# Splitting the projection work between attention steps into parts of two matmuls, and moving what follows VectorE some steps later

## What is computed

```python
proj = h @ w_in[layer]                       # q | k | v | u | gates
# branch A: 8 heads of 64, blocks of 256 keys, top 3 past blocks per query
gate = einsum('bhqd,bhnd->bhqn', qc, k_mean)
gate = where(arange(nb) < own, gate, NEG_INF)
_, sel = lax.top_k(gate, k_sel)
p = softmax(concat([s_sel, s_own])).astype(v.dtype)
y_a = (p_sel @ v_g + p_own @ v_own) @ w_branch_a
# branch B: trailing means of 2, 4, 8, 16 tokens, minus the token
mixed = window_sum / count - u
y_b = (einsum('bsgc,gcd->bsgd', mixed, w_pool) * pool_scale) @ w_branch_b
x = x + (sigmoid(g0) * y_a + sigmoid(g1) * y_b) @ w_out
```

## Time and profile before

| | |
|---|---|
| median of 3 runs | 2349.37 us (2342.2 to 2542.82) |
| profiled execution, device time | 2344.48 us |
| its span (first to last instruction, slowest core) | 2343.4 us |
| spans of the eight cores | 2335.9 to 2343.4 us |
| mean granted TensorE clock, core 1 | 0.934 |
| busy: TensorE, VectorE, ScalarE | 2000.3, 1254.0, 833.8 us |
| first attention stage (layer 1) | 83.9 to 457 us |
| second attention stage (layer 2) | 1211 to 1592 us |

### The profile page before, as it was taken

How to read it: one execution, slowest core, us unless ns; L and a number is a source line. 1 busy time by engine, 2 the same in 40 slices (tenths; PEclk the granted TensorE clock), 3 DMA queues, 4 the chain that set the end, 5 groups by cost and what they waited for, 6 DMA issues and landing times.

```text
span 2343.4 us, 32398 instructions; the slowest of 8 cores (2335.9 to 2343.4 us)
## 1 busy us (share of the span) xinstructions
PE 2000.3 (85%) x12288; PEld 978.8 (42%) x12288; DVE 1254.0 (54%) x1700; ACT 833.8 (36%) x1015; POOL 124.9 (5%) x240
## 2 busy tenths in 40 slices
PE   1867766899999899899996777779999899999987
PEld 1534433444444344344463434334445444444434
DVE  3534333243468748758773324333336785685776
ACT  3344444522234304224434443443223441340443
POOL 1000000000000000000010000000000000000000
PEclk9988887899999999999998878769999999999999
DMA  8101010022132222222130010102222322223213
GB/s 203 19 5 19 1 19 10 5 41 41 28 42 36 32 37 34 35 40 31 15 58 5 1 19 1 18 10 32 37 33 32 45 33 36 36 28 45 33 18 144
DMA packets 38663, 79.60 MB, mean 34 GB/s; under 512 B 4320, under 2 KB 8544, under 8 KB 38496
## 3 DMA queue, kind: packets, MB, share of 16 engines
q0 software_dynamic: 33760, 60.39, 18.2%
q1 hardware_dynamic: 4752, 17.15, 2.2%
HBM read 129.51 MB, written 8.39 MB: 59 GB/s over the span
## 4 chain that ended last, share of the span: by engine, by line
PE 71%; DVE 13%; ACT 7%; issue 6%; DMA 2%; SPq 0%; DVEq 0%; ACTq 0%
PE ps L467 38%; PE ps L912 12%; DVE tv L894 4%; PE ps L858 4%; PE ps L703 4%; ACT Pt L721 4%; PE ps L738 3%; PE ps L808 2%; PE ps L805 2%; PE ps L501 2%; ACT tv L890 2%; DMA xs<-xt 2%; DVE hs L462 1%; DVE tA L576 1%; DVE kz L488 1%
## 5 line engine op out<-in xcount | busy, mean ns | idle before, releaser
L467 PE MATMUL ps<-hs,ring 128*128 128x512 bf16 x4608 | 1097.0, 397 | 59.3 <-DVE tv L894 46.3
L467 PEld LDWEIGHTS ps<-hs,ring 128*128 128x128 bf16 x4608 | 462.8, 102 | 653.5 <-issue 170.8
L912 PE MATMUL ps<-hid,ring 128*128 128x512 bf16 x1408 | 311.9, 383 | 16.5 <-DVE hid L903 15.1
L721 ACT ACTIVATE Pt<-ps 128x1024 bf16<-128x1024 f32 x320 | 271.8, 894 | 90.4 <-PE ps L703 33.3
L894 DVE SCALAR_TENSOR_TENSOR tv<-ps,pv,tv 128x1024 f32<-128x1024 f32 (+2 forms) x176 | 225.8, 1283 | 118.9 <-ACT tv L890 109.4
L738 PE MATMUL ps<-Vt,Pt 128*128 128x65 bf16 x2176 | 132.2, 205 | 152.7 <-ACT Pt L721 146.1
L894 DVE SCALAR_TENSOR_TENSOR tg<-ps,pv,tg 128x1024 f32<-128x1024 f32 (+2 forms) x176 | 225.0, 1279 | 32.5 <-ACT tg L890 22.9
L912 PEld LDWEIGHTS ps<-hid,ring 128*128 128x128 bf16 x1408 | 138.0, 99 | 185.3 <-issue 26.6
L703 PE MATMUL ps<-qz,kz 72*128 72x512 bf16 (+3 forms) x640 | 206.2, 397 | 10.5 <-DVE qz L657 10.5
L738 PEld LDWEIGHTS ps<-Vt,Pt 128*128 128x128 bf16 x2176 | 110.6, 106 | 241.3 <-issue 224.2
L900 ACT ACTIVATE tg<-tg 128x1024 f32<-128x1024 f32 x88 | 93.1, 1058 | 317.7 <-DVE tg L894 317.6
(11 more groups left out here) (78 smaller groups left out, 1299.4 us busy)
## 6 DMA issues: line engine op xcount, KB each, us to landing
ring<-w_up POOLq DMA_DIRECT2D x88, 256.0 KB, 3.8
ring<-w_in POOLq DMA_DIRECT2D x64, 256.0 KB, 4.5
xs<-xt SPq DMA_DIRECT2D x16, 512.0 KB, 27.0
yt<-yst SPq DMA_DIRECT2D x16, 512.0 KB, 2.6
ring<-w_down POOLq DMA_DIRECT2D x32, 224.0 KB, 3.6
ring<-w_ab POOLq DMA_DIRECT2D x16, 256.0 KB, 4.6
ring<-w_out POOLq DMA_DIRECT2D x16, 256.0 KB, 4.7
ring<-w_down POOLq DMA_DIRECT2D x16, 256.0 KB, 3.8
```

The costliest lines, as they stand in the source:

```text
L467: S.op("pe", lambda e: [e.matmul(bank(b), w[:, kc, :], hs[:, c, kc, :], start=(kc == 0), stop=(kc == 7)) for kc in range(8)][-1], reads=[r ...
L721: S.op("act", lambda e: e.activation(Pt[:, pi, 0:n], ps[:, sl * 1024:sl * 1024 + n], AF.Exp, scale=0.125), reads=[PB[2 * sl], PB[2 * sl + ...
L912: S.op("pe", lambda e: [e.matmul(bank(b), w[:, kc, :], hid[:, kc, c * 512:(c + 1) * 512], start=(kc == 0), stop=(kc == nk - 1)) for kc in ...
```

## The change

Each `q`, `k`, `v` and `u` unit is now four parts (`pieces`, `mm8_part`, `proj_v_part`): two matmuls of 512 columns each, or eight of 128 for `v`. The parts of a unit fill one bank over some steps; only behind the last part do the copies out of the bank follow, on the same engines as before. A part counts 0.45 and a `gA` 0.4, and a window's parts are spread by the scores of each step (0.5 plus scores/1024), so a small step gets half as much as a full one. The windows are also filled differently: 6 `u` units now stand in the pairs 0 to 2 and 10 in pair 3, where they were 9 and 7; in pair 3 VectorE copies `u` out of the bank instead of ScalarE.

What depends on VectorE goes on a list (`later`) and is issued by `run_due` some steps on, just before `values(s)`: the sums of `u`, two instructions a step; the ranking in three groups on the three steps after `gA`; `um` two steps after `mx`, `gB` two steps after the ranking, `tr` three steps (not two) after the head's end. One entry of the list with TensorE work is issued in a step. These short tasks use the bank that the latest unit doesn't (`short_bank`).

```diff
 def m1_plan():
-    cnt = [(0, 1, 2), (0, 1, 2), (0, 1, 2), (2, 2, 3)]
+    cnt = [(0, 0, 2), (0, 0, 2), (0, 0, 2), (3, 3, 4)]
...
-COST = {"gA": 0.8, "gB": 0.3, "q": 1.73, "k": 1.73, "v": 1.8, "u": 1.95}
...
+        def mm8_part(b, w, rw, c, lo, hi):
+            S.op("pe", lambda e: [e.matmul(bank(b), w[:, kc, :], hs[:, c, kc, :],
+                                           start=(kc == 0), stop=(kc == 7)) for kc in range(lo, hi)][-1],
+                 reads=[rw] + R_h[c][lo:hi], writes=[PB[b]])
...
+            def run_due(tag=None, all_=False, pe_too=True):
+
+                used = False
+                for it in list(todo):
+                    if tag is not None:
+                        ok = it[1] == tag
+                    else:
+                        ok = all_ or (it[0] <= now[0] and not (it[2] and (used or not pe_too)))
+                    if ok:
+                        todo.remove(it)
+                        used = used or it[2]
+                        it[3]()
...
+                ops.append(mixin)
+                for k, f in enumerate(ops):
+                    later(1 + k // 2, "ud", False, f)
...
+                    later(2, "gB%d" % c, True, lambda: gate_b(m, c))
+                for k, f in enumerate((compare, ties, choose)):
+                    later(1 + k, "gd", False, f)
...
+                    mm8_part(b, w, rw, c, 2 * k, 2 * k + 2)
+                    if k < 3:
+                        return
+                    if kind == "u":
+                        u_done(m, c, b, now[0] >= 120)
+                        return
...
+                return [(0.45, lambda k=k: part(k)) for k in range(4)]
...
-                        trq.append([s + 2, tr])
+                        later(3, "tr", True, tr)
...
-                    q = list(plan[m][w])
-                    tot = sum(COST[t[0]] for t in q)
+                    q = [p for t in plan[m][w] for p in pieces(t)]
+                    room = [0.5 + sum(x[2] for x in steps[40 * m + s][5]) / 1024.0 for s in range(a, z)]
+                    tot = sum(p[0] for p in q)
                     for s in range(a, z):
-                        starts[40 * m + s] = (q, tot * (z - 1 - s) / (z - a))
+                        when[40 * m + s] = (q, tot * sum(room[s - a + 1:]) / sum(room))
```

More of the change, by code:

```diff
@@ L185, in m1_plan @@
     ut = [(g, c) for g in (3, 2, 1, 0) for c in range(NCH)]
-    cnt = [(0, 1, 2), (0, 1, 2), (0, 1, 2), (2, 2, 3)]
+    cnt = [(0, 0, 2), (0, 0, 2), (0, 0, 2), (3, 3, 4)]
     for m in range(4):
-        def us(n):
-            return [("u",) + ut.pop(0) for _ in range(n)]
+        us = [[("u",) + ut.pop(0) for _ in range(n)] for n in cnt[m]]
+        nxt = m + 1 if m < 3 else None
         w0 = [("gA", m, 2)]
@@ L192, in m1_plan @@
             w0.append(("q", m, 3))
[L193 to L206, removed]
+        if nxt:
+            w0 += [("v", nxt, 0), ("v", nxt, 1)]
+        w0 += us[0][:1] + [("gA", m, 3)] + us[0][1:]
+        if nxt:
+            w0.append(("v", nxt, 2))
+        w1 = []
+        if nxt:
+            w1 += [("v", nxt, 3)] + [("k", nxt, c) for c in range(NCH)]
+        w1 += us[1]
+        w2 = [("q", nxt, c) for c in range(3)] if nxt else []
+        w2 += us[2]
         segs.append((w0, w1, w2))
     return segs
-COST = {"gA": 0.8, "gB": 0.3, "q": 1.73, "k": 1.73, "v": 1.8, "u": 1.95}
 def load_order():
@@ L498, in fn @@
                 ins = None
-                for t4 in range(4):
+                for t4 in range(lo, hi):
                     for kc in range(8):
@@ L521, in mixer, with long_bank, short_bank, later @@
             fctr = [0]
-            def fb():
+            now = [0]
+            todo = []
+            def long_bank():
                 fctr[0] += 1
                 return 6 + fctr[0] % 2
+            def short_bank():
+                return 6 + (fctr[0] + 1) % 2
+            def later(n, tag, pe, fn):
+                todo.append((now[0] + n, tag, pe, fn))
+            def run_due(tag=None, all_=False, pe_too=True):
[9 more added lines that the diff above has]
+                        it[3]()
             for st in range(2):
@@ L659, in gate_b, with pieces, part @@
                          reads=[PB[b]], writes=[R_q[c]])
[L661 removed]
+            def pieces(t):
                 kind = t[0]
[L663 to L675 removed]
+                if kind == "gA":
+                    return [(0.4, lambda: gate_a(t[1], t[2]))]
+                m, c = t[1], t[2]
+                box = []
+                def part(k):
+                    if k == 0:
+                        box.append(long_bank())
+                    b = box[0]
+                    if kind == "v":
+                        proj_v_part(l, m, c, b, k, k + 1)
+                        return
+                    w, rw = W(l, kind, m)
+                    mm8_part(b, w, rw, c, 2 * k, 2 * k + 2)
+                    if k < 3:
+                        return
+                    if kind == "u":
+                        u_done(m, c, b, now[0] >= 120)
+                        return
                     if c == 3:
@@ L753, in tr @@
                         def tr():
[L754 removed]
+                            b = short_bank()
                             trb = bank(b).bitcast(BF16)
@@ L779, in mixer @@
                 attend(s)
-                while trq and trq[0][0] <= s:
-                    trq.pop(0)[1]()
-                if s in starts:
-                    q, left = starts[s]
-                    while q and sum(COST[t[0]] for t in q) > left + 1e-6:
-                        task(q.pop(0))
+                if s in when:
+                    q, left = when[s]
+                    while q and sum(p[0] for p in q) > left + 0.2:
+                        q.pop(0)[1]()
+                run_due()
                 values(s)
-            while pend_um:
-                pend_um.pop(0)()
-            while trq:
-                trq.pop(0)[1]()
+            while todo:
+                run_due(all_=True)
             heir("mg", ["kqv"])
```

130 lines of the change are left out of this document (65 added, 65 removed).

## The result

The changed kernel takes **2149.26 us** (median of 4 runs, 2148.25 to 2149.9). Against the kernel before on the same chip the ratio is **0.9162** (95% interval 0.9137 to 0.9186): 8.4% faster. The profiled execution took 2149.47 us, 195 us less than the one before.

A forecast was written before the change was run, and what follows sets the result against it. Attention stages were taken as bound by TensorE's waits and lower clock, no engine being full. Work 405.6 + waits 126 + clock 29 = 561 us for 754, so 2344.5 - 194 = 2150 us; range 2100 to 2240.

The forecast's parts named there:

- run-out: A TensorE matmul before a wait shows its full run-out: 0.15 us for each of some 165 waits before, 25 us.
- work at full clock: TensorE's work in both attention stages, start to start at full clock: 405.6 us, the same matmuls after the change.
- values waiting for Exp: TensorE's values waiting in the attention stages: 66 us behind `q` and `k` units, 10 behind `u`, 31 behind `um`.
- all other waits: TensorE's remaining waits in both stages: `gA` 8 x 1.0, `gB` and scores behind it 6 x 1.0, stages' ends 5: 19 us.
- lower clock: Time both stages lose to TensorE's reduced clock: 118 us before; most should go, a quarter, 29 us, is kept.
- rival B: Waits only move: ScalarE's order is the true bound and short tasks wait for banks; 2336 us, chance 0.07.
- The copies of `u` moved to VectorE: 20 of 32 `u` copies go to VectorE, adding 14 us of work there; costed at 0, as VectorE is busy 36%.
- The `q` and `k` holes: Behind each of 48 units the 2.84 us copy-and-Exp chain stays, more matmuls cover it: mean wait 1.37, 66 us for 103.
- the term of 31 us: Values behind `um`: a chain of 2.33 us against 1.34 of cover, 0.99 us for each of 32.
- 312 signals: Units issued in four operations signal 312 times more: taken as 0; by the Trainium skill 8 us higher.
- Rival A: The clock doesn't come back: waits fall as forecast but the 118 us of lower clock stay; 2240 us, chance 0.14.
- C: Slower, as the lower clock becomes lasting: the stages run at 0.50 and take 831 us; 2421 us, chance 0.05.

The follow-up runs named there:

- ScalarE first: Changed kernel, but ScalarE copies the first head of each `q` or `k` unit and VectorE the second: 2122.52 us, ratio 0.9048.

## What the prediction had right, and the step that failed

The forecast was 2150 us and 194 us of gain; measured were 2149.3 and, in the profiled executions, 195. The mechanism is shown: the chain behind a unit stays, the parts cover it, and the clock follows. That the total came out to 1 us is luck, for the waits were mis-sized both ways, by some 40 us, and cancel. By the prediction's own reckoning, with 0.15 us of run-out for each of the 133 waits:

| term, both stages | before | predicted | measured |
|---|---|---|---|
| work at full clock | 405.6 | 405.6 | 405.6 (the same instructions) |
| values waiting for Exp | | 107 | 56.7 + 10 = 67 |
| all other waits | | 19 | 52.0 + 10 = 62 |
| waits together | 231 | 126 | 129 |
| lower clock | 118 | 29 | 20 (what is left) |
| stages | 754 | 561 | 555 |

**The step that failed** is the term of 19 us for all other waits: they took 52.0 us idle and some 62 with run-out. The 68 waits behind it, in idle us of both stages, against what the prediction had for them:

| wait of TensorE | predicted | measured |
|---|---|---|
| `gA` for the casts of the key sums, 8 | 8 | 10.0 |
| `gB` for the bank of a `v` unit, 8; scores behind a `gB`, none | 6 | 4.1 |
| at the stages' ends, 4 | 5 | 3.4 |
| `tr` for the bank of a `q` unit that ScalarE still copies, 6 | 0 | 7.1 |
| `um` and parts behind VectorE's queue in pair 3, 8 | 0 | 10.2 |
| a part or a short task whose bank the last short task's reader still holds, 34 | 0 | 16.4 |

What the prediction priced came out near its price. It put at nothing that parts and short tasks share banks 6 and 7, so that each waits until the one before it in its bank is read. It argued that few short tasks stand in the step in which a unit ended, and priced such waits in rival B alone; the trace has 40 of them (the fourth and the last line), of 0.2 to 1.7 us. And it took VectorE as covered because it is busy 36% on the mean. That is the mean of a stage: at the start of pair 3, where ranking, sums, copies and divisions meet, VectorE was the bound. Most of the 40 are not of this kind: in some 18 of their 23.5 us the reading engine had been idle and began at once, and TensorE waited for as long as the reading lasts. The copies of `u` moved to VectorE were costed at 0, with a gain of some 16 us on ScalarE's side, and gave nothing, since on ScalarE they leave no wait for an Exp either.

**The `q` and `k` holes**: the chain stays, its cover grows. Right, shown from both sides: without the parts the waits for Exp are back at 62 us a stage, and with ScalarE first the wait shrinks by 0.9 us, the VectorE copy of 0.68 and its hand-over. The size was too large: 66 us predicted for 48 holes; 36 of the units have a wait of values behind them, 41.7 us idle and 47 with run-out. They run from 0.69 to 1.76 us, against 0.88 to 1.74 predicted, so one hole was sized well and their number wasn't: behind six more units it is the `tr` above that waits.

**`um`**: the term of 31 us was too large. Values wait behind 17 of the 32, 0.3 to 1.0 us each, 9.6 us in all:

```profile
329.13 0.38 PE L627 MATMUL ps<-mx,wpl 128*128 128x512 bf16 x1
329.61 0.69 ACT L629 ACTIVATE pooledT<-ps,pv 128x512 bf16<-128x512 f32 x1 [0.55 <-PE ps L627]
330.19 1.93 ACT L774 ACTIVATE Pt<-ps 128x1024 bf16<-128x1024 f32 x2
330.44 0.59 PE L468 MATMUL ps<-hs,ring 128*128 128x512 bf16 x2 [0.25 <-ACT pooledT L629]
331.35 0.41 PE L791 MATMUL ps<-Vt,Pt 128*128 128x65 bf16 x8 [0.32 <-ACT Pt L774]
```

The chain is 2.22 us as priced (2.33), but here the wait is 0.57 in two places. Behind the others no value waits for its Exp.

**The work** and the signals: taken as 0, and right. The 8 us that the prediction held against the split for 312 signals are not there, by the unit of 1.73 us with four signals above.

**The clock**: most of the 118 us came back, as predicted; a quarter was kept for what turned out to be a sixth. The 20 us are what is left of the sum, and the granted clock agrees: at 0.95 and 0.96 some 50 us of the stages run at the lower level, where the same work takes twice the time, so by estimate up to 25 us. Where the clock is still lost TensorE had mostly waited for VectorE just before. At the start of pair 1:

```profile
148.94 0.34 PE L650 MATMUL ps<-ksb,qz 72*128 72x8 bf16 x8 [1.39 <-DVE ksb L642]
149.75 0.59 PE L468 MATMUL ps<-hs,ring 128*128 128x512 bf16 x2 [0.48 <-DVE gm L656]
```

From 151.2 us on the clock is at its lower level. Seven of the eleven times at which it falls in the two stages stand like this one behind a `gA`, two behind a late `um` in pair 3. Rival A and C fall with a clock of 0.95. Rival B falls too, but its mechanism, short tasks held by a bank, is what the failed term lacked.

The order also leaves step 1 of pair 0 and step 7 of pair 3 without a part, not only the last step of a pair, as the prediction had it; no wait of note stands there.

## What to carry to other kernels

Look for the longest chain between two dependent pieces of the pacing engine, and count what it has to do meanwhile: cutting large units so that some of the next one always stands behind the end of the last one is worth the cover that it adds. Then shorten the chain itself, which is often cheaper: swapping which engine reads a bank first gave 27 us here after the change, and 90 us before it. When the pacing engine gets faster, an engine with a low mean load can become the bound where its work bunches; spread that by place, not by stage. And price each hand-over of a shared bank: 40 short ones of 0.2 to 1.7 us came to 23.5 us here, where the sum had nothing.

## What the runs showed of the hardware that was not expected

Waits of 2 us, repeated every few microseconds, can cost more through TensorE's clock than by themselves. In the kernel before, 35 us less idle time made the stages 94 us shorter at a clock of 0.90 for 0.80 to 0.83.

In the changed kernel waits of up to 1.5 us behind `q` and `k` units, between steps that nearly all hold some projection, left the clock at 1.00 for 64 us on end, while it fell behind the waits of 1.39 and 0.48 us of a `gA`:

```profile
151.00:155.00 4.00, 4.00 (x29) 2.21 (x27) 3.53 (x8) 1.63 (x3) 0.00 (x0) 0.57 0.00 0
155.00:219.00 64.00, 51.09 (x599) 31.43 (x596) 28.16 (x63) 39.62 (x49) 2.11 (x4) 1.00 0.05 8
```

So the length of a single wait does not tell whether the clock falls. Which property of the stretch does is not shown.
